# One-pass matmuls that walk their stream and their PSUM output backwards

## The chip, the cores and the metric

The kernel runs on one core of a Trainium2 chip. The metric is the device time of one execution in microseconds (us); lower is better. The core has TensorE (PE in the profile, its weight loads PEld), VectorE (DVE), ScalarE (ACT), GpSimd (POOL) and SyncE (SP). Matmuls read their operands from SBUF and write to PSUM, which has eight banks of 512 float32 columns in each of 128 partitions.

## The reference

A two-layer trunk over 1024 tokens of width 1024, with 16 learned meta tokens put in front (L = 1040). The first layer mixes with a gated delta rule, the second with stick-breaking attention against shared keys and values; each is followed by a gated feed-forward of inner width 2816.

```python
for layer in range(DEPTH):                      # DEPTH = 2
    if layer < N_A_LAYERS:                      # layer 0
        h = h + gdn_mixer(rms_norm(h, ...), gdn_w_in, ..., gdn_w_out)
    else:                                       # layer 1
        h = h + sb_mixer(rms_norm(h, ...), k_sh, v_sh, w_q, w_o)
    h = h + swiglu(rms_norm(h, ...), ffn_w_gate_up, ffn_w_down)
    if layer == N_A_LAYERS - 1:
        k_sh, v_sh = shared_kv(h, kv_norm_g, w_kv)
return rms_norm(h, final_norm_g)[:, N_META:]

def swiglu(h, w_gate_up, w_down):
    gu = h @ w_gate_up
    return (jax.nn.silu(gu[..., :D_FF]) * gu[..., D_FF:]) @ w_down
```

The change concerns the dense products `h @ w`: the input projection (1024 to 4096 and 16 more), the two output projections, the key/value and query projections, and both feed-forwards.

## The kernel before, in words

Activations lie transposed: features on the 128 partitions, tokens along the columns. A dense product of float32 precision is made of three one-pass products. Weights and activations are each split into a high and a low part of type F32R (`WH`, `WL`, `RH`, `RL`; `YH`, `YL`, `XH`, `XL`, `QP` for the streams), and low x high, high x low and high x high are added up in one PSUM bank. For each of them a 128x128 weight tile is loaded (an LDWEIGHTS on PEld) and the activations are streamed past it as the moving operand, one PSUM column per column of the stream. Sums, transposes and most of the delta rule use plain float32 matmuls.

There are three places in which the program issues such triples on TensorE:

- `chunk` (L2396 to L2398): input projection (32 jobs), output projection of the delta-rule mixer and of the attention (8 jobs each). A job is 128 output features over 8 k-tiles. The tokens are cut into chunks: three of 348, 346 and 346 columns (`ALL_CH`, starts 0, 348 and 694), or two of 512 in the attention's output projection (`SEQ_CH`).
- `mill`, in its `product` (L2831, or L2833 and L2834): both feed-forwards. A Strassen-like scheme makes seven products from each pair of 2x2 blocks; `STEPS` is the list of 238 products in the order in which they run, over 924 k-tiles in all. In the second layer one product streams 512 columns into one bank (L2831). In the first layer it streams 520, as two halves of 260 into two banks with a weight load each (L2833 and L2834).
- `project`, in its `tile` (L2960 to L2962): key/value projection (16 jobs, three chunks) and query projection (8 jobs, two chunks of 512).

Each engine has its own program, written out in order, and waits on semaphores that others raise. Around the products stand: ScalarE rounds weights to their high part (L1511, L1238, L1243), VectorE takes the low part (L2132, L1764), GpSimd adds weight blocks (L1141); behind them VectorE takes the sums out of PSUM (L2166, L1839, L2336, L2204). A product's last matmul raises the semaphore that VectorE waits for. Before a bank is used again, TensorE waits until it was read.

Three other rows come up. L2854 is a sum of squares in the second feed-forward, a plain float32 matmul of 512 columns with `ones` as its weights. L2290 is the running product of the stick-breaking attention, a scan on VectorE that walks its tile from the last column to the first (`P_of(U)[:, 0:n][:, ::-1]`). L2917 is the last of a group of 128-column transposes.

Of the kernel before, what the change touches and what calls it, by code (L numbers as in the profile page):

```python
# [11 lines left out]
KT = D // 128  # L12
# [163 lines left out]
TILE_ORDER = [0, 1, 2, 3, 4, 5, 7, 6]  # L176
# [35 lines left out]
def trunk(nc, x, meta_tokens, gdn_norm_g, gdn_w_in, gdn_conv_w, gdn_a_log, gdn_dt_bias, gdn_onorm_g,  # L212
# [23 lines left out]
    with ctx:  # L236
# [161 lines left out]
        def y_high(t):  # L398

            return YB[:, t - 4, 0, :] if t in (4, 5) else YA[:, t if t < 4 else t - 2, 0, :]  # L400
# [1987 lines left out]
        def _(pe):  # L2388
            def chunk(s, bank, t0, n, hi=YH, low=YL, late=None):

                for k in range(KT):
                    if late and k == KT - 1:
                        pe.wait_ge(*late)
                    wh, wl = WH[s][:, 128 * k:128 * k + 128], WL[s][:, 128 * k:128 * k + 128]
                    xh, xl = hi[:, k, t0:t0 + n], low[:, k, t0:t0 + n]
                    pe.matmul(PS[:, bank, 0:n], wl, xh, start=(k == 0), stop=False)  # L2396
                    pe.matmul(PS[:, bank, 0:n], wh, xl, start=False, stop=False)  # L2397
                    m = pe.matmul(PS[:, bank, 0:n], wh, xh, start=False, stop=(k == KT - 1))  # L2398
                m.then_inc(mm_chunk, 1)

            def turn_in(i):
# [406 lines left out]
            def mill(m):  # L2808

                ph = m.before  # L2810

                def product(n):

                    p, i = STEPS[n]
                    q, kn, acc, cols = X_OF[i], tiles_of(p), m.acc(n), m.hn // m.halves
                    pe.wait_ge(*since(m.f_lo, n + 1))
                    for w in acc_free(n):
                        pe.wait_ge(*w)
                    if operand_of_step(n):
                        c, i = operand_of_step(n)  # L2820
                        pe.wait_ge(*since(m.d_lo, 7 * c + REFILL_ORDER.index(i) + 1))
                    for k in range(kn):
                        if p == 0 and i in (0, 2, 6):
                            pe.wait_ge(*since(m.q_lo, {0: 0, 2: 4, 6: 8}[i] + k + 1))
                        elif p == 0 and k == 0:
                            pe.wait_ge(*since(m.q_lo, {1: 13, 3: 14, 4: 15, 5: 16}[i]))
                        wh, wl = m.RH[n % m.ring][:, k, :], m.RL[n % m.ring][:, k, :]
                        xh, xl = m.parts(m.q_high(q, k, 1)[:, 0, :]), m.parts(m.q_low(q, k, 1)[:, 0, :])
                        for w, x, first, last in ((wl, xh, k == 0, False), (wh, xl, False, False), (wh, xh, False, k == kn - 1)):
                            if m.halves == 1:  # L2830
                                done = pe.matmul(acc, w, x, start=first, stop=last)  # L2831
                            else:
                                pe.matmul(acc[:, 0, :], w, x[:, 0, :], start=first, stop=last)  # L2833
                                done = pe.matmul(acc[:, 1, :], w, x[:, 1, :], start=first, stop=last)  # L2834
                    done.then_inc(m.f_mm[0], 1)

                def drained(n):

                    return since(m.f_d, READ_OUT[n]) if STEPS[n][1] else since(m.f_t, STEPS[n][0] + 1)

                def acc_free(n):

                    taken0 = TAKEN0[ph]
                    if m.layer:
                        return [drained(n - 8)] if n >= 8 else {2: [(taken, taken0 + 16)], 6: [(ssln, R0[ph] + 2)]}.get(n, [])
                    if n < 4:
                        return [(taken, taken0 + (12, 20, 22, 24)[n])]
                    return [drained(n - 2)] if n < 6 else [(ssln, R0[ph] + n - 5)] if n < 8 else [drained(n - 4)]

                def half_total(h):  # L2850

                    pe.wait_ge(acc_r, ACC0[ph] + ph.nch * 7 - (0 if m.layer == 0 or h else 1))
                    if m.layer:
                        pe.matmul(m.total(h), ones[:, :], m.sum_of[h], start=True, stop=True).then_inc(ss_r, 1)  # L2854
                    else:
                        pe.wait_ge(*drained(h))
                        for s in range(2):
                            done = pe.matmul(m.total(h)[:, s, :], ones[:, :], m.parts(m.sum_of[h])[:, s, :], start=True, stop=True)
                        done.then_inc(ss_r, 1)

                for n in range(len(STEPS)):
                    product(n)
                    if m.layer and n == len(STEPS) - 2:
                        final(0)
                        final(1)
                    if n == 3:
                        half_total(0)
                        half_total(1)
# [85 lines left out]
            def project():  # L2954

                def tile(s, bank, t0, n, t):

                    wh, wl = WH[s][:, 128 * t:128 * t + 128], WL[s][:, 128 * t:128 * t + 128]
                    xh, xl = y_high(t)[:, t0:t0 + n], y_low(t)[:, t0:t0 + n]
                    pe.matmul(PS[:, bank, 0:n], wl, xh, start=(t == TILE_ORDER[0]), stop=False)  # L2960
                    pe.matmul(PS[:, bank, 0:n], wh, xl, start=False, stop=False)
                    return pe.matmul(PS[:, bank, 0:n], wh, xh, start=False, stop=(t == TILE_ORDER[-1]))  # L2962

                def total_kv(ch):

                    n = ALL_CH[ch][1]
                    pe.wait_ge(acc_r, ACC0[P_KV] + 3 * ch + 3)
                    if ch == 2:
                        pe.wait_ge(ssln, R0[P_KV] + 1)
                    pe.matmul(PS[:, 6 + ch % 2, 0:n], ones[:, :], sqb[:, ch % 2, 0, 0:n], start=True, stop=True).then_inc(ss_r, 1)  # L2970

                for l in range(P_KV.jobs + P_Q.jobs):
                    ph, m = (P_KV, l) if l < P_KV.jobs else (P_Q, l - P_KV.jobs)
                    pe.wait_ge(w_lo, P_KV.job0 + l + 1)
                    if ph is P_Q and m == 1:
                        pe.wait_ge(taken, TAKEN0[P_Q])
                    if ph is P_Q and m == P_Q.jobs - 1:
                        scores(0)
                        scores(1)
                        turn_values(0, 2)  # L2980
                        pe.wait_ge(t_ca, 2)
                    if l == 1:
                        pe.wait_ge(*since(mills[0].f_d, READ_OUT[len(STEPS) - 1]))
                    if l == 0:
                        for ch, (t0, n) in enumerate(ph.chunks):
                            pe.wait_ge(*since(mills[0].f_d, READ_OUT[len(STEPS) - (2 if ch == 2 else 3)]))
                            for t in TILE_ORDER[0:6]:
                                if ch == 0:
                                    pe.wait_ge(y_lo, Y0[P_KV] + TILE_ORDER.index(t) + 1)
                                tile(6, ch, t0, n, t)  # L2990
                        for ch, (t0, n) in enumerate(ph.chunks):
                            for t in TILE_ORDER[6:8]:
                                if ch == 0:
                                    pe.wait_ge(y_lo, Y0[P_KV] + TILE_ORDER.index(t) + 1)
                                done = tile(6, ch, t0, n, t)
                            done.then_inc(mm_chunk, 1)
                        continue
                    for ch, (t0, n) in enumerate(ph.chunks):
                        if ph is P_Q and m == P_Q.jobs - 2 and ch:
                            turn_values(0, 0)  # L3000
                            turn_values(0, 1)
                        if ph is P_Q and m == P_Q.jobs - 1 and ch:
                            scores(2)
                            pe.wait_ge(t_ca, 3)
                        if m >= 2:
                            pe.wait_ge(taken, TAKEN0[ph] + ph.nch * (m - 2) + ch + 1)
                        for t in TILE_ORDER:
                            done = tile(6 + l % 4, ph.nch * (m % 2) + ch if ph is P_KV else q_bank(m, ch), t0, n, t)
                        done.then_inc(mm_chunk, 1)
                        if l == 1:  # L3010
                            total_kv(ch)
# [59 lines left out]
```

## Time and profile before

| what | value |
|---|---|
| device time, three runs | 2789.69, 2791.95, 2792.91 us (median 2791.95) |
| profiled execution: span from first to last instruction | 2787.4 us |
| mean granted TensorE clock (share of full speed) | 0.995 |
| TensorE matmul, busy | 2724.4 us, 19450 matmuls |
| weight loads, busy | 2492.4 us |
| VectorE, busy | 1988.4 us |
| ScalarE, GpSimd, busy | 1071.9 us, 1218.3 us |

Of the profiled execution the span is what the profile gives; the time of a run holds that and what lies around the first and the last instruction. Matmuls overlap: the duration of one is longer than the time from its start to the start of the next, so that the busy time of TensorE is that in which at least one is under way.

### The profile page before, as it was taken

The numbers are of one execution on the slowest core, as the hardware profiler recorded it, in microseconds if no ns is written. First come the engines' busy times: TensorE is split into PE (matmuls) and PEld (weight loads), VectorE is DVE, ScalarE is ACT, GpSimd is POOL, SyncE is SP. The second block draws the span as 40 slices with busy tenths as digits, with TensorE's granted clock in tenths as the row PEclk, the third lists the DMA queues.
The fourth block names the chain that finished last, engine by engine and source line by source line (L and its number), as shares of the span: only waits on it lengthen the run. The fifth ranks groups of instructions, "written<-read, shape, count | busy, mean of one in ns | idle before, by whom it ended". The sixth has DMA issues, their size and how long they took to land. (4 is left out here: it accounts for less than half of the span.)

```text
span 2787.4 us, 48746 instructions
## 1 busy us (share of the span) xinstructions
PE 2724.4 (98%) x19450; PEld 2492.4 (89%) x19450; DVE 1988.4 (71%) x2502; ACT 1071.9 (38%) x1994; POOL 1218.3 (44%) x1056
## 2 busy tenths in 40 slices
PE   8999999999999999999999999999999999999998
PEld 7999998888999999999999998788887888887886
DVE  6777536887468777777778444577747888888788
ACT  5222224544443332333434101477744333334333
POOL 3000015566146555565563000233223666665775
PEclk9999999999999999999999999999999999999999
DMA  4333332231302222234431425555320232335432
GB/s 124 92 93 84 92 126 99 94 117 61 96 5 100 100 103 100 88 130 164 154 127 54 145 99 167 159 122 119 85 61 31 98 111 86 110 106 189 166 132 91
DMA packets 215995, 298.40 MB, mean 107 GB/s; under 512 B 9915, under 2 KB 151372, under 8 KB 215772
## 3 DMA queue, kind: packets, MB, share of 16 engines
q1 hardware_dynamic: 205194, 257.01, 29.5%
q0 software_dynamic: 10368, 38.21, 4.0%
q8 instruction: 156, 2.56, 0.4%
q14 instruction: 67, 0.55, 0.1%
q10 hardware_dynamic: 210, 0.07, 0.0%
HBM read 212.08 MB, written 83.19 MB: 106 GB/s over the span
## 5 line engine op out<-in xcount | busy, mean ns | idle before, releaser
L2132 DVE TENSOR_TENSOR RL<-RAW,RH 128x512 fp32r<-128x512 f32 (+1 forms) x408 | 413.0, 1014 | 197.3 <-ACT RH L1511 196.4
L1511 ACT ACTIVATE RH<-RAW 128x512 fp32r<-128x512 f32 (+1 forms) x408 | 248.3, 617 | 667.5 <-POOL RAW L1141 244.3
L2831 PE MATMUL PS<-QP,RH 128*128 128x512 f32 x1584 | 489.0, 390 | 0.0
L2834 PE MATMUL PS<-QP,RH 128*128 128x260 f32 x1584 | 415.2, 283 | 0.0
L2833 PE MATMUL PS<-QP,RH 128*128 128x260 f32 x1584 | 415.0, 283 | 0.0
L2831 PEld LDWEIGHTS PS<-QP,RH 128*128 128x128 f32 x1584 | 298.1, 188 | 62.1 <-issue 0.2
L2831 PE MATMUL PS<-QP,RL 128*128 128x512 f32 x792 | 310.2, 392 | 6.6 <-DVE RL L2132 4.8
L2833 PEld LDWEIGHTS PS<-QP,RH 128*128 128x128 f32 x1584 | 300.4, 190 | 0.0
L2834 PEld LDWEIGHTS PS<-QP,RH 128*128 128x128 f32 x1584 | 299.8, 189 | 0.0
L1141 POOL TENSOR_TENSOR RAW<-RAW 128x512 f32<-128x512 f32 (+1 forms) x136 | 209.0, 1538 | 155.3 <-DVE RL L2132 150.0
L2396 PE MATMUL PS<-YH,WL 128*128 128x348 f32 (+1 forms) x744 | 241.7, 325 | 2.5 <-DVE WL L1764 2.5
L2398 PE MATMUL PS<-YH,WH 128*128 128x348 f32 (+1 forms) x744 | 239.9, 322 | 0.0
L2397 PE MATMUL PS<-YL,WH 128*128 128x348 f32 (+1 forms) x744 | 239.5, 322 | 0.0
L2833 PE MATMUL PS<-QP,RL 128*128 128x260 f32 x792 | 225.2, 284 | 11.6 <-DVE RL L2132 5.2
L2834 PE MATMUL PS<-QP,RL 128*128 128x260 f32 x792 | 224.6, 284 | 0.0
L2831 PEld LDWEIGHTS PS<-QP,RL 128*128 128x128 f32 x792 | 149.1, 188 | 41.2 <-DVE RL L2132 6.6
L1006 POOL DMA_DIRECT2D s_in<-obuf x32 | 30.8, 961 | 332.1 <-ACT obuf L1297 332.1
L1141 POOL TENSOR_TENSOR RAW<-TS,RAW 128x512 f32<-128x512 f32 (+1 forms) x68 | 88.2, 1297 | 184.4 <-DVE RL L2132 183.9
L2166 DVE TENSOR_TENSOR ua<-PS,ua 128x520 f32<-128x520 f32 (+1 forms) x240 | 160.7, 683 | 5.1 <-PE PS L2831 5.0
L2166 DVE TENSOR_TENSOR sg<-PS,sg 128x520 f32<-128x520 f32 (+1 forms) x240 | 161.3, 684 | 3.9 <-DMA s_a<-sg 2.6
L2833 PEld LDWEIGHTS PS<-QP,RL 128*128 128x128 f32 x792 | 150.1, 189 | 13.5 <-issue 7.3
L2834 PEld LDWEIGHTS PS<-QP,RL 128*128 128x128 f32 x792 | 149.8, 189 | 0.0
(374 smaller groups left out, 6953.1 us busy)
## 6 DMA issues: line engine op xcount, KB each, us to landing
RAW<-in_ffn_w_gate_up SPq DMA_DIRECT2D x44, 1024.0 KB, 5.2
s_in<-obuf POOLq DMA_DIRECT2D x32, 520.0 KB, 4.4
raw<-in_gdn_w_in SPq DMA_DIRECT2D x32, 512.0 KB, 4.1
RAW<-in_ffn_w_down SPq DMA_DIRECT2D x16, 1024.0 KB, 5.3
QF<-s_a SPq DMA_DIRECT2D x12, 1040.0 KB, 8.3
QF<-s_a SPq DMA_DIRECT2D x12, 1024.0 KB, 7.2
s_a<-ua SPq DMA_DIRECT2D x22, 520.0 KB, 2.8
s_a<-ua SPq DMA_DIRECT2D x22, 512.0 KB, 3.3
```

The costliest lines, as they stand in the source:

```text
L1006: pool.dma_start(s_in_w[t:t + 1].rearrange("t p c j -> p (t c) j"), obuf[:, j % 2, :].rearrange("p (c j) -> p c j", j=C)).then_inc(stored[ ...
L1141: pool.tensor_tensor(out, a, b, op).then_inc(m.f_sum[0], 1)
L1511: act.activation(m.RH[n % m.ring][:, 0:kn, :], m.weight_block(p, i), ACT.Copy).then_inc(m.f_hi[0], 1)
L2132: dve.tensor_tensor(m.RL[n % m.ring][:, 0:kn, :], m.weight_block(p, i), m.RH[n % m.ring][:, 0:kn, :].bitcast(F32), ALU.subtract).then_inc( ...
L2166: dve.tensor_tensor(m.parts(m.out_block(p, w)), z, m.parts(m.out_block(p, r)), ALU.add).then_inc(m.f_d[0], 1)
L2396: pe.matmul(PS[:, bank, 0:n], wl, xh, start=(k == 0), stop=False)
L2397: pe.matmul(PS[:, bank, 0:n], wh, xl, start=False, stop=False)
L2398: m = pe.matmul(PS[:, bank, 0:n], wh, xh, start=False, stop=(k == KT - 1))
L2831: done = pe.matmul(acc, w, x, start=first, stop=last)
L2833: pe.matmul(acc[:, 0, :], w, x[:, 0, :], start=first, stop=last)
L2834: done = pe.matmul(acc[:, 1, :], w, x[:, 1, :], start=first, stop=last)
```

## The change

In the three places the moving operand and the PSUM output are sliced with `[:, ::-1]`. Column n-1 of the stream goes first and lands in column n-1 of the bank, column 0 goes last; the sums in PSUM are the same. The weights are read as before. In the built program 13,116 matmuls have the step -1 on both sides, all with F32R operands. The instructions of all engines and their order are the same as before.

```diff
             def chunk(s, bank, t0, n, hi=YH, low=YL, late=None):
...
-                    xh, xl = hi[:, k, t0:t0 + n], low[:, k, t0:t0 + n]
-                    pe.matmul(PS[:, bank, 0:n], wl, xh, start=(k == 0), stop=False)
-                    pe.matmul(PS[:, bank, 0:n], wh, xl, start=False, stop=False)
-                    m = pe.matmul(PS[:, bank, 0:n], wh, xh, start=False, stop=(k == KT - 1))
+                    xh, xl = hi[:, k, t0:t0 + n][:, ::-1], low[:, k, t0:t0 + n][:, ::-1]
+                    z = PS[:, bank, 0:n][:, ::-1]
+                    pe.matmul(z, wl, xh, start=(k == 0), stop=False)
+                    pe.matmul(z, wh, xl, start=False, stop=False)
+                    m = pe.matmul(z, wh, xh, start=False, stop=(k == KT - 1))
...
                             if m.halves == 1:
-                                done = pe.matmul(acc, w, x, start=first, stop=last)
+                                done = pe.matmul(acc[:, ::-1], w, x[:, ::-1], start=first, stop=last)
                             else:
-                                pe.matmul(acc[:, 0, :], w, x[:, 0, :], start=first, stop=last)
-                                done = pe.matmul(acc[:, 1, :], w, x[:, 1, :], start=first, stop=last)
+                                pe.matmul(acc[:, 0, :][:, ::-1], w, x[:, 0, :][:, ::-1], start=first, stop=last)
+                                done = pe.matmul(acc[:, 1, :][:, ::-1], w, x[:, 1, :][:, ::-1], start=first, stop=last)
...
                 def tile(s, bank, t0, n, t):
...
-                    xh, xl = y_high(t)[:, t0:t0 + n], y_low(t)[:, t0:t0 + n]
-                    pe.matmul(PS[:, bank, 0:n], wl, xh, start=(t == TILE_ORDER[0]), stop=False)
-                    pe.matmul(PS[:, bank, 0:n], wh, xl, start=False, stop=False)
-                    return pe.matmul(PS[:, bank, 0:n], wh, xh, start=False, stop=(t == TILE_ORDER[-1]))
+                    xh, xl = y_high(t)[:, t0:t0 + n][:, ::-1], y_low(t)[:, t0:t0 + n][:, ::-1]
+                    z = PS[:, bank, 0:n][:, ::-1]
+                    pe.matmul(z, wl, xh, start=(t == TILE_ORDER[0]), stop=False)
+                    pe.matmul(z, wh, xl, start=False, stop=False)
+                    return pe.matmul(z, wh, xh, start=False, stop=(t == TILE_ORDER[-1]))
```

## Rows read from the trace of the kernel before

**Rows 1.** The page's head, busy times, and busy tenths in 40 slices.

```profile
span 2787.4 us, 48746 instructions
...
PE 2724.4 (98%) x19450; PEld 2492.4 (89%) x19450; DVE 1988.4 (71%) x2502; ACT 1071.9 (38%) x1994; POOL 1218.3 (44%) x1056
...
PE   8999999999999999999999999999999999999998
...
DVE  6777536887468777777778444577747888888788
ACT  5222224544443332333434101477744333334333
POOL 3000015566146555565563000233223666665775
PEclk9999999999999999999999999999999999999999
```

**Rows 2.** Windows: first feed-forward, key/value projection, second feed-forward.

```profile
core 0: us, PE busy (x) PEld busy (x) DVE busy (x) ACT busy (x) POOL busy (x), PEclk, DMA share, GB/s
900.00:1250.00 350.00, 350.00 (x2924) 350.00 (x2923) 261.15 (x316) 107.12 (x176) 208.25 (x140) 1.00 0.30 102
1550.00:1650.00 100.00, 100.00 (x631) 100.00 (x630) 43.01 (x61) 13.85 (x13) 6.88 (x13) 1.00 0.35 122
2250.00:2550.00 300.00, 300.00 (x1325) 248.48 (x1324) 257.58 (x284) 99.73 (x160) 192.32 (x128) 1.00 0.35 118
```

**Rows 3.** Groups of TensorE's matmuls by line and shape.

```profile
line engine op names shapes xcount | busy us, mean ns | idle before us <-releasers
L2831 PE MATMUL PS<-QP,RH 128*128 128x512 f32 x1584 | 489.0, 390 | 0.0
L2834 PE MATMUL PS<-QP,RH 128*128 128x260 f32 x1584 | 415.2, 283 | 0.0
L2833 PE MATMUL PS<-QP,RH 128*128 128x260 f32 x1584 | 415.0, 283 | 0.0
...
L2398 PE MATMUL PS<-YH,WH 128*128 128x346 f32 x496 | 159.3, 321 | 0.0
...
L2960 PE MATMUL PS<-YA,kWL 128*128 128x346 f32 x192 | 62.1, 323 | 0.0
...
L2854 PE MATMUL PS<-sg,ones 128*128 128x512 f32 x4 | 1.9, 591 | 0.0
```

**Rows 4.** Groups of VectorE's instructions by line and shape.

```profile
L2290 DVE TENSOR_TENSOR_SCAN PB<-PB 128x1040 f32<-128x1040 f32 x16 | 37.2, 2324 | 12.4 <-POOL PB L1207 12.4
...
L2290 DVE TENSOR_TENSOR_SCAN PB<-PB 128x912 f32<-128x912 f32 x16 | 32.7, 2041 | 10.7 <-POOL PB L1207 10.7
...
L2301 DVE TENSOR_TENSOR partL<-obuf 128x1039 f32<-128x1039 f32 x8 | 9.8, 1231 | 0.0
```

**Rows 5.** Timeline of TensorE in the attention: start, duration, engine, line.

```profile
2001.43 0.27 PE L2915 MATMUL PS<-ident,PS 128*128 128x128 f32 x1
2001.54 0.27 PE L2917 MATMUL PS<-ident,PS 128*128 128x128 f32 x1
```

## The prediction

> **What bounds the kernel now.** I read the page's first two parts first. TensorE's matmul row is busy for 98% of the span, VectorE for 71% and the others for less than half, and the slices show no stage in which another engine stands at nine tenths beside an idle TensorE [rows 1]. So any time added to or taken from a typical matmul reaches the end almost undiminished: TensorE has 2787.4 - 2724.4 = 63.0 us of idle time in the whole span, and only that much could swallow a loss.
>
> A matmul's own duration does not say how fast the stream of them goes, since matmuls overlap. The second view is therefore the table of windows, three long stretches that hold one width of product each and in which TensorE is never idle [rows 2]. Dividing length by count gives the time from one product to the next:
>
> - first feed-forward, 260 columns: 350.00 us / 2924 = 119.7 ns
> - second feed-forward, 512 columns: 300.00 us / 1325 = 226.4 ns
> - key/value projection, 348 or 346 columns (346.7 on average over a job's three chunks): 100.00 us / 631 = 158.5 ns
>
> The granted clock is 1.00 in all three, the upper level of 2.4 GHz. Two of the widths give the price of a column: (226.4 - 119.7) / (512 - 260) = 0.4235 ns. What is left is a fixed share for each product: 119.7 - 260 x 0.4235 = 9.6 ns, the same at 512 columns, and 158.5 - 346.7 x 0.4235 = 11.7 ns at the middle width. The durations say the same of a column: 390 against 283 ns is 107 ns for 252 columns [rows 3], 0.425 ns each.
>
> **The change, part by part.** It touches three places, and in each the moving operand and the PSUM output get a step of -1. Weights, widths, banks, order, waits and semaphores are left as they are. No engine gets an instruction more or less and no wait is added, so nothing moves behind or in front of anything; the only price is a new one per column or per product. What it touches, counted from the program's loops:
>
> - the feed-forward stages have 924 k-tiles of three products each: 2772 of 512 columns in the second layer, and twice as many, 5544 of 260, in the first, whose products are cut in two
> - input, output and key/value projections over three chunks: (32 + 8 + 16) jobs x 8 x 3 x 3 = 4032 of 346.7 columns
> - query projection and attention output over two chunks: (8 + 8) x 8 x 3 x 2 = 768 of 512 columns
>
> That is 13,116 of the 19,450 matmuls on the page, and 5544 x 260 + 4032 x 346.7 + 3540 x 512 = 4.652 million columns. By the intervals above they take 5544 x 119.7 + 4032 x 158.5 + 3540 x 226.4 ns = 664 + 639 + 801 = 2104 us, three quarters of the span; 4.652 million x 0.4235 ns = 1970 us of it is columns and 134 us the fixed shares.
>
> No row of before shows a TensorE product with a descending stream, so the price is bounded from both sides.
>
> Upper end, per column: the nearest row in which a 512-column matmul is slower is the sum of squares in the second feed-forward, which streams the same shape as plain float32 and not in the one-pass format: 591 ns against 390 [rows 3]. That is 201 / 512 = 0.39 ns more per column, nearly a second column time. If a descending column cost that, the sum would be 4.652 million x 0.39 = 1814 us. Rows in which a step of -1 runs at all are on VectorE: the attention's scans walk their tile backwards, 2324 - 2041 = 283 ns for 128 columns, 2.21 ns each, against 1231 ns for 1039 columns of a forward subtraction, 1.18 ns each [rows 4]. The ratio of 1.9 is of the same size, but a scan also needs its last result for the next one, so the row cannot tell direction from that.
>
> Upper end, per product: if turning from the last column of one stream to the first of the next cost as much again as the fixed share does now, the sum would be 134 us.
>
> Lower end: a gain can only come out of the fixed share. A transpose of 128 columns starts 0.11 us after the one before it [rows 5], so a narrow matmul does not come down to 128 x 0.4235 = 54 ns; if the weight load sets that, 260 columns at 119.7 ns can give back no more than some 9.7 ns. All fixed shares together are the 134 us.
>
> I take zero. The reason is in rows 3: products of 346 columns last 321 ns whether they read the input projection's operand or the key/value stage's (323), with starts at columns 348 and 694 of a row, and the two halves of a 260-column pair both last 283 ns, although one starts at column 0 of its operand's row and the other at column 260. Where in a row or a bank a stream begins has no price that the trace shows; the column step has, and 0.42 ns is what one column per clock gives at the upper level. A descending stream touches the same columns, two neighbours one after the other as before, and every width is even, so that a bank's columns still come in the same pairs.
>
> Here the Trainium skill speaks against me. The page "PSUM — Partial Sum Buffer", in Specifications (TRN2), says that PSUM is accessed in 8-byte lines, two float32 values, and that a non-contiguous access pattern slows matmuls significantly; "Advanced Engine Details and Errata", Memory Cachelines, asks that every two consecutive elements be contiguous for best throughput, and for SBUF two hits in a 16-byte line. Read by lines, a step of -1 still hits each line twice, and the sum by that is zero; read strictly, a descending pattern is not contiguous, and the sum is that of the first rival. No run here shows which reading holds.
>
> So the sum is 0 us on 2787.4. The profiled execution's span is 2.3 to 5.5 us below the times of the three runs, whose median of 2791.95 us holds what lies around the span. I predict 2792 us. One part in 500, 5.6 us, is about what a measurement of this kernel can tell from no change; spread over 13,116 products that is 0.43 ns each, one column time.
>
> **The rivals.**
>
> *Half rate.* The write or the read of a descending stream moves one column where two went, and every product in all three places grows by about a column time per column. The price is 1814 us by the float32 row and 1970 us by doubling the column; TensorE's 63 us of idle time, which lies where it waits for VectorE's weight parts, is the most that would be hidden. That gives 2792 + 1814 - 63 = 4543 to 2792 + 1970 = 4762 us. For it: the backward scans and the strict reading of the pages. Against it: nothing but that the neighbours stay neighbours. Chance 0.18. It decides from 0.43 ns per product up, so a thousandth of it would already show.
>
> *A turning price.* Columns flow as before, but each product pays some cycles where the stream jumps from one end to the other, or where its address is set up. From 0.43 ns per product (2798 us) up to a doubled fixed share (2926 us). For it: a fixed share exists and I cannot say what it is made of. Against it: in the forward order the address jumps back across the tile just as far between two products. Chance 0.15.
>
> *Faster.* The fixed share shrinks, because the jump from the end of one stream to the start of the next now goes the other way and costs less. The most is 134 us, 2658 us; a nanosecond per product is 13 us, 2779. For it: the share differs between stages, 9.6 against 11.7 ns. Against it: all three products of a k-tile still start on one and the same column, so the jump is as long as before. Chance 0.07.
>
> *The change does nothing.* If the step were undone on both sides when the program is built, nothing would differ; that has the forecast's time and is counted with it.
>
> **How the numbers follow.** No price, or less than 5.6 us: 0.60, at 2792 us, with its own range of 2786 to 2798. The range I give holds this case, the turning price whole (0.15) and nearly all of the faster case, down to 4 ns per product (52 us, 2740): some 0.80 together. Half rate at 0.18 is left out. Its lower end is 2740 and its upper end 2926 with a little room, 2940. Faster 0.07, same 0.60, slower 0.18 + 0.15 = 0.33.
>
> **What the profile of the changed kernel would show.** If I am right, the three stretches hold the same counts within one in a hundred, the durations stay at 283, 321 and 390 ns, TensorE's busy time stays at 2724 us, and the waits of ScalarE and VectorE for its products keep their length. Half rate would show as about half the products in the same 350 us, durations near 591 ns at 512 columns, and VectorE's weight parts long finished before they are wanted, so that the waits of TensorE for them vanish. A turning price would show as one number of nanoseconds, the same at 260, 347 and 512 columns, and would weigh most in the first feed-forward, which has the most products. I am wrong if the hardware pairs columns by an ascending step and not by the line they fall in.

## The result and the profile after

The changed kernel takes 2810.27 us, the median of four runs (2805.48 to 2811.14), against 2791.8 us: a ratio of 1.0065, 95% interval 1.0051 to 1.0079. That is 18.5 us slower. The profiled span is 2808.0 us, 20.6 us longer.

The page's head and first part, the counterpart of [rows 1]:

```profile
span 2808.0 us, 48746 instructions
...
PE 2749.9 (98%) x19450; PEld 2500.4 (89%) x19450; DVE 1985.2 (71%) x2502; ACT 1069.3 (38%) x1994; POOL 1195.0 (43%) x1056
```

TensorE is busy 25.5 us longer with the same instructions. Where, the same three windows show (columns as in [rows 2]):

```profile
900.00:1250.00 350.00, 350.00 (x2925) 350.00 (x2924) 260.42 (x317) 105.71 (x175) 205.31 (x140) 1.00 0.29 101
1550.00:1650.00 100.00, 100.00 (x627) 100.00 (x626) 45.09 (x63) 14.90 (x14) 7.94 (x15) 1.00 0.37 128
2250.00:2550.00 300.00, 300.00 (x1287) 241.71 (x1286) 243.58 (x280) 92.29 (x154) 172.61 (x125) 1.00 0.31 105
```

The clock is the same, 1.00 in all three. At 260 columns 2925 products fit where 2924 did: no price. At 346.7 columns it is 627 for 631, 159.5 ns for 158.5. At 512 columns it is 1287 for 1325, 233.1 ns for 226.4. The groups by shape, to be held against [rows 3], say it in durations, 398 for 390, 324 for 321, 285 for 283 ns:

```profile
L2832 PE MATMUL PS<-QP,RH 128*128 128x512 f32 x1584 | 500.9, 398 | 0.0
L2835 PE MATMUL PS<-QP,RH 128*128 128x260 f32 x1584 | 415.7, 285 | 0.0
...
L2399 PE MATMUL PS<-YH,WH 128*128 128x346 f32 x496 | 160.6, 324 | 0.0
...
L2855 PE MATMUL PS<-sg,ones 128*128 128x512 f32 x4 | 1.9, 592 | 0.0
```

The last row, plain float32 and not turned, is unchanged from 591. The second feed-forward as a whole, from the start of its first product to the start of its last (columns: window, its length, TensorE busy and matmuls, clock, DMA share, GB/s), before and after:

```profile
2127.30:2772.10 644.80, 636.75 (x2793) 1.00 0.34 115
```

```profile
2133.90:2792.70 658.80, 653.78 (x2793) 1.00 0.33 112
```

It is 14.0 us longer, 17.0 us by TensorE's busy time, since its idle time in there falls from 8.1 to 5.0 us. The other 6.6 us of the 20.6 have been lost by the time the stage begins, 2133.9 for 2127.3: 3.4 us before the first feed-forward's first product and 3.0 us between the two feed-forwards.

### The profile page after: what moved, and what is told of

It is laid out like the page before. It is cut to its first block and busy times, and to the rows that moved or that the text cites. A ratio compares the mean times of both kernels' runs of the same rounds, so it can differ in the third digit from the quotient of the medians.

```text
span 2808.0 us, 48746 instructions
## 1 busy us (share of the span) xinstructions
PE 2749.9 (98%) x19450; PEld 2500.4 (89%) x19450; DVE 1985.2 (71%) x2502; ACT 1069.3 (38%) x1994; POOL 1195.0 (43%) x1056
## 5 line engine op out<-in xcount | busy, mean ns | idle before, releaser
L2832 PE MATMUL PS<-QP,RH 128*128 128x512 f32 x1584 | 500.9, 398 | 0.0
L2832 PE MATMUL PS<-QP,RL 128*128 128x512 f32 x792 | 316.4, 399 | 4.3 <-DVE RL L2132 3.2
L2832 PEld LDWEIGHTS PS<-QP,RL 128*128 128x128 f32 x792 | 149.3, 189 | 43.3 <-DVE RL L2132 5.0
L2834 PEld LDWEIGHTS PS<-QP,RL 128*128 128x128 f32 x792 | 149.9, 189 | 14.0 <-issue 7.4
L2397 PEld LDWEIGHTS PS<-YH,WL 128*128 128x128 f32 x744 | 141.0, 190 | 10.6 <-issue 7.4
```

Of the source, the lines that this page charges most:

```text
L2397: pe.matmul(z, wl, xh, start=(k == 0), stop=False)
L2832: done = pe.matmul(acc[:, ::-1], w, x[:, ::-1], start=first, stop=last)
L2834: pe.matmul(acc[:, 0, :][:, ::-1], w, x[:, 0, :][:, ::-1], start=first, stop=last)
```

## The experiments

Two theories stood after this. By the first (W in what follows) a backward column costs and only a wide product shows it; by the second (T) each product pays for turning, 18.5 us / 13,116 = 1.4 ns. A third (N) blamed the neighbours, engines and DMAs on the same memories.

**A quiet chip, all widths.** A small kernel loads a tile, then lets TensorE stream triples alone, with nothing else running:

```diff
+for b, w, x, f, _ in triples(3):      # once for each width n; all four forms in turn
+    done = pe.matmul(PS[:, b, 0:n], w, x[:, 0:n], **f)
+    done = pe.matmul(PS[:, b, 0:n][:, ::-1], w, x[:, 0:n][:, ::-1], **f)
+    done = pe.matmul(PS[:, b, 0:n], w, x[:, 0:n][:, ::-1], **f)
+    done = pe.matmul(PS[:, b, 0:n][:, ::-1], w, x[:, 0:n], **f)
```

> The kernel computes nothing of the reference: it copies x to the output and streams one-pass products on a quiet chip, 72 of each kind, at widths from 128 to 512, forwards, backwards on both sides, backwards in the read alone, backwards in the PSUM write alone. Theory W (a backward column costs, and a wide product shows it): at 512 the backward product takes some 6 to 8 ns more from start to start than the forward one, at 346 some 1 to 3, at 260 and below nothing. Theory T (a turning price for each product): the same 1.4 ns at every width from 260 up. Theory N (neighbours: a backward stream only loses where other engines and DMAs use the memories): no difference over 1 ns at any width here. The two one-sided stretches tell which side pays; if the PSUM write pays, the stretch with the read alone turned stays at the forward time.

The view of a line gives count, durations (smallest, median, largest) and the first and last start. One of the three products of each triple, 512 columns: forwards, both sides turned, read turned, write turned.

```profile
L143 PE MATMUL PS<-H,WL x24: 387/392/396, 549.5 to 565.5; 128*128 128x512 f32 x24
```
```profile
L145 PE MATMUL PS<-H,WL x24: 397/398/398, 566.2 to 582.4; 128*128 128x512 f32 x24
```
```profile
L147 PE MATMUL PS<-H,WL x24: 397/398/398, 583.1 to 599.3; 128*128 128x512 f32 x24
```
```profile
L149 PE MATMUL PS<-H,WL x24: 390/392/396, 600.0 to 616.0; 128*128 128x512 f32 x24
```

The read pays and the write does not: turned in the write alone, the stretch is as long as the forward one, 16.0 us; with the read turned it is 16.2 us. Start to start over all 72 products of a form (last start less first start, through 71; the starts are given to 0.1 us, so 1.4 ns is the step), in ns:

```
columns    forwards   both   read   write
   128       111.3   111.3  111.3   111.3
   260       119.7   121.1  119.7   119.7
   346       160.6   160.6  159.2   159.2
   384       174.6   177.5  177.5   174.6
   448       202.8   207.0  207.0   201.4
   512       232.4   235.2  235.2   232.4
```

The turning price falls with this: 346 columns pay nothing here. The neighbours are not needed. In the same run a stream of 480 columns that starts 2 columns on takes 221.1 ns forwards for 218.3, and a PSUM output that starts 2 columns on leaves 218.3. But the backward price at 512 is 2.8 ns and not the 6.7 of the kernel or the 6 to 8 expected, and what differs from the kernel is the forward time, 232.4 and not 226.4. So the question became what makes a forward product of one and the same width cost 226 or 232 ns.

**Wide or narrow products alone**, in the whole kernel:

```diff
-                    xh, xl = hi[:, k, t0:t0 + n][:, ::-1], low[:, k, t0:t0 + n][:, ::-1]
-                    z = PS[:, bank, 0:n][:, ::-1]
+                    d = -1 if n == 512 else 1          # the other kernel: n < 512
+                    xh, xl = hi[:, k, t0:t0 + n][:, ::d], low[:, k, t0:t0 + n][:, ::d]
+                    z = PS[:, bank, 0:n][:, ::d]
```

(likewise in the other two places).

> Only products of 512 columns run backwards (3540 of 13116). Theory W: 2805 to 2811 us, practically the whole loss. Theory T (1.4 ns each): 3540 x 1.4 = 5 us, 2797 us. Theory N gives no number by width: the loss goes with the stages that are busy in memory, and since the second feed-forward holds most of these products it could be the whole too.

> Only products of 260, 346 and 348 columns run backwards (9576 of 13116). Theory W: 4032 x 1 to 3 ns = 4 to 12 us at most, less what the idle time takes, and nothing from the 5544 products of 260 columns: 2793 to 2800 us. Theory T: 9576 x 1.4 = 13 us, 2805 us.

Wide alone: 2806.01 against 2790.51 us, 1.0055 (1.0043 to 1.0068), 15.5 us. Narrow alone: 2792.73, 1.0015 (1.0005 to 1.0024), 2.2 us. The two together give 17.7 us of the 18.5, and the 3540 wide products, a quarter of all, hold seven eighths of it. That is the first theory's split; turning would have put 13 us into the narrow ones.

**Read or write alone in the second feed-forward.** The products of the other stages run forwards:

```diff
-                                done = pe.matmul(acc, w, x, start=first, stop=last)
+                                done = pe.matmul(acc, w, x[:, ::-1], start=first, stop=last)   # the other kernel: acc[:, ::-1], w, x
```

> Only the 2772 products of the second feed-forward read backwards; PSUM is written forwards, so their columns come out mirrored and the output is not the reference's. If the read pays alone, as the quiet chip shows: 2802 to 2807 us, 0.4 to 0.6 per cent over before, 1287 products in the 300 us of the second feed-forward. If the write pays in this kernel: before's time.

> Only the 2772 products of the second feed-forward write PSUM backwards and read forwards; their columns come out mirrored and the output is not the reference's. If the read pays alone: before's time within 0.2 per cent and 1325 products in the 300 us. If the write pays in this kernel: 2802 to 2807 us.

Read: 2804.2 against 2790.09 us, 1.0047 (1.0033 to 1.0061), 14.1 us. Write: 2789.84, 1.0000 (0.9990 to 1.0009). The window of the stage, read turned and then write turned:

```profile
2250.00:2550.00 300.00, 300.00 (x1288) 241.70 (x1287) 244.31 (x278) 91.86 (x155) 173.00 (x125) 1.00 0.30 102
```
```profile
2250.00:2550.00 300.00, 300.00 (x1326) 248.47 (x1325) 257.36 (x283) 99.34 (x160) 191.94 (x128) 1.00 0.35 118
```

1288 as in the changed kernel, 1326 as before. The read is the whole of it in the kernel as well.

**Where stream and weights stand.** Groups of twelve products as in the second feed-forward, 512 columns, on the quiet chip (the loop in short):

```diff
+c = w0 + (0 if same else 128 * k)                       # weight tile: w[:, c:c + cols]
+x = S[:, x0 + (2 * k + q) * pitch:x0 + (2 * k + q) * pitch + n]
+pe.matmul(PS[0:cols, g % 8, 0:n], w[:, c:c + cols], x[:, ::d], ...)
```

> The kernel computes nothing of the reference: it copies x to the output and streams groups of twelve one-pass products as the second feed-forward does, 216 of each kind, forwards and with the read alone backwards. Changed are the start of the stream (by 2 to 64 columns), the pitch of the streams (512, 520, 544), the start of the weight tiles (by 16 to 64 columns), the width of the weight tile (128, 64, 32 columns) and whether all twelve share one weight tile per part. Theory L (the stream and the weight load that runs beside it get in each other's way, and how much depends on where both stand in memory): the forward time itself moves by several ns with the start of stream or weights, the backward price moves too and may vanish or change its sign, and with a weight tile of 32 columns both directions come closer together and down. Theory R (a backward read simply costs some 3 to 7 ns per 512 columns): the same price at every start, pitch and weight tile, also with 32 columns of weights.

Start to start over 216 products (through 215, to 0.5 ns), forwards and with the read backwards:

```
                                   forwards  backwards
as the second feed-forward            227.0      233.5
stream 2, 4, 8 columns on      232.1, 232.1, 233.5   235.3, 233.5, 233.5
stream 16, 32, 64 columns on   228.8, 232.6, 227.0   233.5, 233.5, 233.5
weights 16, 32, 64 columns on  233.5, 232.1, 226.5   233.0, 236.7, 233.0
pitch 520, 544                 231.6, 228.8          233.5, 233.5
one weight tile for all               226.5      233.5
weight tile of 64, 32 columns  230.2, 231.6          233.5, 233.0
```

The first line is the kernel's own pair, 226.4 and 233.1, without the kernel. The rows of the two products with the high weights show the same in durations: with nothing moved forwards, the same backwards, and forwards with the weights 32 columns on.

```profile
L55 PE MATMUL PS<-S,RH x144: 389/389/390, 73.1 to 121.6; 128*128 128x512 f32 x144
```
```profile
L57 PE MATMUL PS<-S,RH x144: 395/397/402, 122.0 to 172.0; 128*128 128x512 f32 x144
```
```profile
L95 PE MATMUL PS<-S,RH x144: 390/393/404, 1075.6 to 1125.3; 128*128 128x512 f32 x144
```

So it is the forward product that has a good place, where it takes 2 to 7 ns less than at the other places, and comes back to it after 64 columns, 256 bytes. Half of the theory falls here: a weight tile of 32 columns, a quarter of the load, was to bring both directions down, and it brought the forward time up and left the backward time where it was. A smaller load beside the stream does not make room for it.

**All starts, and both moved together** (again in short):

```diff
+for x0 in range(0, 64, 4): triples(x0=x0, d=1), triples(x0=x0, d=-1)
+for w in (8, 16, 32, 48): triples(x0=w, w0=w, d=1), triples(x0=w, w0=w, d=-1)
```

> The kernel computes nothing of the reference: it copies x to the output and streams groups of twelve products, 216 of each kind, read forwards and backwards, with the stream's start moved in steps of 4 columns from 0 to 60, with stream and weight tiles moved together by 8, 16, 32 and 48 columns, and at 260 and 346 columns. Theory L (place of the stream against the place of the weight tile): moved together, both keep the time of no move, 227 forwards and 233 to 234 ns backwards; forwards the time goes up and down over the 64 columns between 227 and some 234. Theory A (only the stream's own start counts): moved together by 32 columns the forward stream takes 232 to 233 ns as with the stream moved alone. Theory P (a backward stream has a good place too, only another one): some start between 0 and 60 brings the backward time to 227; if there is none, backward reading has lost the good place for good.

Windows of 48 us: forwards and backwards with no move, forwards and backwards with the stream alone 32 columns on, forwards and backwards with both 32 on:

```profile
73.20:121.20 48.00, 48.00 (x213) 1.00 0.00 0
122.20:170.20 48.00, 48.00 (x207) 1.00 0.00 1
875.90:923.90 48.00, 48.00 (x207) 1.00 0.00 0
926.30:974.30 48.00, 48.00 (x207) 1.00 0.00 1
1882.30:1930.30 48.00, 48.00 (x213) 1.00 0.00 1
1931.30:1979.30 48.00, 48.00 (x207) 1.00 0.00 1
```

Moved together, the 213 products are back; it was so at 8, 16 and 48 columns too, 227.0 ns forwards each time. What counts forwards is therefore the place of the stream against that of the weight tile. Alone, the stream's start gives 226.5 ns at 0, 228.8 at 16, 230.7 to 231.6 at 4, 20 and 28, and 233.0 to 236.3 ns at the other eleven. Backwards all sixteen give 233.0 or 233.5: among starts at multiples of four columns a backward read has no good place. The forward times add up product by product: with a pitch of 520 or 544 columns the streams go through several places, and the mean of the times above at those places is 231.6 and 228.8 ns, what the run before measured. At 260 columns forwards is 119.1 ns in the good place and 120.9 with the stream 32 columns on, and backwards 120.0 in both. At 346 columns it is 159.5 and 159.1 forwards and 160.0 backwards in both.

**The loss without a backward step.** In the second feed-forward the weight tiles, and the few tiles behind them, lie 128 bytes further on; once with the kernel before, once with the changed one:

```diff
+                if m.layer:
+                    ff("weight_pad", [128, 32])
                 for s in range(m.ring):
                     m.RH[s] = ff(f"RH{s}", [128, 4, 128], F32R)
```

> All products run forwards as before; in the second feed-forward the weight tiles lie 32 columns (128 bytes) further on, the streams where they were. Theory L: 232.1 ns instead of 226.4, 1293 products in the 300 us of that stage, 2772 x 5.1 to 5.7 ns = 14 to 16 us, 2801 to 2807 us: the loss of the change without any backward step. If the place is of no matter in the kernel: before's time, 1325 products.

> The changed kernel with the weight tiles of the second feed-forward 32 columns further on. Theory L: 236.7 ns instead of 233.5 there, 1267 products in 300 us, 2772 x 3.2 ns = 9 us over the changed kernel, 2815 to 2820 us. If a backward read has one price at every place: the changed kernel's 2806 to 2811 us.

Moved, all forwards: 2800.73 against 2791.71 us, 1.0033 (1.0020 to 1.0046), 9.0 us where 14 to 16 were expected. Moved and backwards: 2812.38 us, 1.0072 (1.0058 to 1.0086), between the two ranges expected, so that the total decides for neither. The stage's window, moved forwards (and the whole stage) and then moved backwards:

```profile
2250.00:2550.00 300.00, 300.00 (x1292) 1.00 0.31 107
2127.90:2781.80 653.90, 649.08 (x2792) 1.00 0.33 113
```
```profile
2250.00:2550.00 300.00, 300.00 (x1287) 1.00 0.31 104
```

1292 products was what the small kernel's 232.1 ns said. TensorE is busy 12.3 us longer in the stage (649.08 - 636.75) and idle 3.2 us less, and the stage is 9.1 us longer: two thirds of what the backward read does to it, with no backward read. By an estimate the place alone costs nearer 9.1 + 1.7 = 10.8 us, and 12.3 + 1.7 = 14.0 us of busy time, the lower end of what was expected. In the profile of before the granted clock fell once in this stage, to 0.83 over the 10 us from 2570, which is worth some 1.7 us, after TensorE had been idle for 3.6 us; the changed kernel has such a stretch too (0.85), and the moved one, idle for 2.4 us at the same point, has none.

```profile
2570.00:2580.00 10.00, 8.19 (x29) 0.83 0.13 48
```

Turning the read on top of that takes the window from 1292 to 1287 only, 0.9 ns for each product instead of 6.7. The small kernel's 236.7 ns for this place backwards did not come back here; the kernel stayed at 233.1 ns, as it does without the move, so for the backward read theory L was wrong. The quiet chip says so too: stream or weights moved 32 columns give the same place against each other, and forwards the same 232 to 233.5 ns, but backwards 233.5 and 236.7.

## Why the prediction was right in its range and wrong in its likeliest case

**The range and the side.** 2810 us lies in 2740 to 2940, by the turning price, to which I gave 0.15; that the range holds it is luck, since the mechanism behind that part of it is not what happened. The likeliest case, no price, is out: the loss is three times what I called measurable. The turning price had the size, 18.5 us within 2798 to 2926, but not the mechanism: it was to be the same in ns at every width and to weigh most in the first feed-forward. That stage lost nothing (2925 products for 2924 in the window, 683.1 us for 682.9 from the first start to the last), and the 512-column products of the second feed-forward lost 6.7 ns each.

**The step that failed is "I take zero", and in it the sentence that where a stream begins has no price that the trace shows.** I looked at 260 and 346 columns, where that is nearly so (1.8 and 0.4 ns between two places on the quiet chip). At 512 the profile of before holds this row, which I did not read:

```profile
L2398 PE MATMUL PS<-XH,WH 128*128 128x512 f32 x128 | 50.3, 393 | 0.0
```

393 ns in the attention's output projection against 390 in [rows 3] for the same shape, before anything was turned. Its streams have a pitch of 1040 columns, so they stand differently against their weights from k-tile to k-tile. After the change these rows are 396 and 398. In 82 us of the output projection, before and after:

```profile
2045.00:2127.00 82.00, 82.00 (x356) 1.00 0.17 52
```
```profile
2051.00:2133.00 82.00, 82.00 (x352) 1.00 0.17 52
```

That is 230.3 ns forwards and 233.0 backwards: the same turn costs 2.7 ns here and 6.7 ns in the second feed-forward. With a pitch of 1040 columns the place moves on by 16 columns from one k-tile to the next; if the tiles lie as the program declares them, the streams go through the places 0, 16, 32 and 48, and the small kernel's times there average 230.6 ns. A forward product in the second feed-forward was cheap because of its place, the backward read had no such place at any start tried, and what the change costs there is that saving.

**The price by column.** The upper bounds by column, 0.39 and 0.4235 ns, were thirty times the largest price seen: 6.7 / 512 = 0.013 ns. That every column or every product should pay alike, as these rivals had it, was wrong too. The interval of 226.4 ns, which I split into 0.4235 ns per column and a fixed 9.6 ns, was not of two clean parts: on the quiet chip the same 512 columns take 226.5 to 236.3 ns forwards.

**The write.** Here the reasoning held: neighbours stay neighbours and pairs stay pairs, and a backward write costs nothing (1.0000). Of the two readings of the page "PSUM — Partial Sum Buffer", Specifications (TRN2), in the Trainium skill the strict one is not borne out for a step of -1. For the read the same reasoning failed: its columns too came two neighbours one after the other, and it paid 6.7 ns. Half rate, at 0.18, never came near.

**Cover.** TensorE's idle time hid little, as said: 3.0 of the 17.0 us in the second feed-forward. TensorE's waits for VectorE's weight parts shrink there, as the half-rate rival would have had it, and by a few us.

**The rest.** The narrow products' 2.2 us fit 4032 products of 1.0 ns, 4 us, less some cover; on the quiet chip 346 columns pay 0.5 to 0.9 ns. That the 5544 products of 260 columns pay nothing agrees with the quiet chip, where backwards lies between the forward times of two places, 120.0 between 119.1 and 120.9 ns; that the first feed-forward averages over such places was not tried.

**What stays open.** Why the place of the stream against the weights counts, and why only forwards, is not shown: the runs give the distances, not what meets there. Starts that are no multiple of four columns were tried once only (2 columns on: 235.3 ns backwards), and none at which the column that a backward stream reads first, its last one, stands where the weight tile's first column does; a good place for backward reads there is not ruled out. The first small kernel, whose streams lie 544 columns apart from one k-tile to the next, is 2 ns above what the places explain, 232.4 for a mean of 230.0, and its backward products are at 235.2; that was not followed up.

## What to carry to other kernels

The order in which a matmul walks PSUM was free here, and the order in which it reads SBUF was not; try the two apart before a layout needs one of them. Compare all rows of one shape across stages before calling a dependence nil: three nanoseconds between two 512-column rows pointed to the cause here. Where wide one-pass products run back to back, the place of the stream against its weight tile is worth a look: 32 columns of padding cost 0.33% of this kernel, and any new tile in front of the weights could do so by accident.

## What the hardware showed that I had not expected

A forward 512-column product next to a 128-column weight load takes 226.5 ns when stream and weight tile start at the same place within 256 bytes, and 228.8 to 236.3 ns at the other starts tried; moving both together changes nothing. The page "TensorE: Matmul & The Clock Gate" of the Trainium skill (Part 2, Step-by-step: what each phase is for) has two separate SBUF read ports, so that loading the next weights takes no read bandwidth from the running matmul. The measurement differs so far as the place of the weight tile alone moved the stream from 227.0 to 232.1 ns; that bandwidth is what is taken, no run shows.
